# A decoder trunk on eight cores: the attention's first query tile in its second part, an earlier state load, and a background thread in single steps

## The chip, the cores and the metric

The kernel runs on the 8 cores of one Trainium2 chip. Each core takes one prompt of 2048 tokens and four sample sequences of 4 tokens (16 sample tokens), so the cores do the same work on different data and don't exchange anything. The metric is the device time of one launch, that of the slowest core, in microseconds; lower is better.

Engines: TensorE (PE) multiplies matrices and writes PSUM, which has 8 banks of 128 partitions x 512 fp32 numbers. ScalarE (ACT) and VectorE (DVE) read PSUM and SBUF. GpSimd (POOL) does small arithmetic here and issues DMAs that convert fp32 to bf16 or gather rows; SyncE (SP) only issues DMAs. Each engine works through its own instructions in order and waits on semaphores for the others.

## The reference, cut to what matters

Four layers follow each other: short gated convolution (A0), sparse attention (B), a gated recurrence (C), and a short convolution again (A1). Every layer is `x = LayerNorm(ALPHA * x + mixer(x))`.

```
# short conv: h, b, c, z = split(x @ w_in)
conv, new_buf = causal_dwconv(c_gate * h, buf, conv_w)   # buf: conv states
return (silu(z) * b_gate * conv) @ w_out, new_buf

# attention, per query block: three branches of keys
o_c = softmax(q k_c) v_c      # keys compressed by 32
o_s = softmax(q k_s) v_s      # the 16 blocks of 64 with the highest scores
o_w = softmax(q k_w) v_w      # the last 512 keys
y = ((g0*o_c + g1*o_s + g2*o_w) * silu(z)) @ w_out
```

For the sample tokens the compressed and selected keys come from a paged cache of 8192 rows per sequence. The results are the two outputs, the new key and value rows, and the new states.

## The kernel before, in words

**Order and dependencies.** The program is written out in order, and a small framework (`FW`) adds the waits. Every tile has one or more `Buf` records with its last writer and its readers; `FW.op` and `FW.dma` make the issuing engine wait for whatever an instruction reads or overwrites. A second DMA that writes under the same `Buf` therefore waits on its queue until the first has landed. Weights come through a ring of three tiles of 8 x 128 x 512 (`wtile`, `_issue_w`), loaded by POOL as soon as the tile that held the slot is used up.

**Layer A (`layer_A`).** For each of 8 column blocks c, and each of 4 token tiles of 512 and a small one of 16, TensorE computes four products (L560), each into a bank that `ps()` hands out in rotation: seven banks in A0, since bank 7 belongs to the page compression. ScalarE copies or activates two of them (L566, L567), VectorE does the convolution (L583 to L591). At the head of the layer `st_in`, the conv states (`sconv`, 32 KB), is loaded by SP, and ScalarE copies it into `exs` by eight instructions (L542), its first ones in the program. In A0 the generator `compress_pages` runs along: 32 pages of the sample cache are gathered by POOL into two buffers `PG` (L627), multiplied on VectorE with the weight table `WT` (L640) and summed on TensorE (L651, L653). Its setup code, which runs when the generator is made, puts four loads on the queues; that of `WT` (`s_cWT`) is held back on SP until the fourth tile of x (`xb[(0, 3)]`) has landed.

**Layer B, projections (`b_project`)** leave the queries in `G`, head pair c in `G[:, c, :]`: head c of group g=0 on partitions 0 to 63, of g=1 on 64 to 127.

**Layer B, attention (`b_attention`).** The work is a list of items. Part `ph` = 0 has query tiles QT = 0 and 1, part 1 has 2 and 3; in each part c runs over the 8 head pairs, and for each c the units (QT, g) run in the order (0,0) (0,1) (1,0) (1,1), or (2,0) (2,1) (3,0) (3,1). A unit's keys are cut into banks of 512 columns by `unit_banks`, and two banks are one item. The units have 3, 3, 7, 6 and 9, 8, 11, 10 items, so a c has 19 items in part 0 and 38 in part 1. For an item `scores` issues the products of keys and queries (L1251, L1244 for the compressed keys, L1255 for masks) into one of two PSUM pairs, and ScalarE takes the exponential of up to 1024 columns (L1260). Two items later `outputs` multiplies with the values (L1308) into the third or fourth pair, `psum2[2 + u % 2]` for the unit's number u. At a unit's end VectorE normalises from PSUM (L1331 to L1342). When g is 1, four transposes (L1346) into the same pair follow three items later, and VectorE copies them to `G` (L1348), over the queries that are used up. In part 0 an item "imp" is put in after the third item of (1,0) for each c (and one more at c = 6): scores of the compressed keys for 128 queries of tiles 2 and 3, and on VectorE the choice of the 16 best blocks (`importance`, L1272 to L1292). At c = 7 the item "nmt" transposes the eight results into masks, and four DMAs put them into the mask rows of the part-1 query tiles.

**Query tiles.** `QA[s_][g]`, with s_ = 2*ph + c%2, holds for one c the queries of a part (copied from `G` by SP), constants (`qc`, by POOL, converting) and the mask rows. `load_q` for the next c is emitted at the start of each c.

**Layer B, after the attention.** The z products: 8 blocks m x 5 token tiles (L933), Silu on ScalarE (L939), product into `G` on VectorE (L941). A second generator, `sample_bg`, does the sample tokens' attention in the background. `pump(k)` runs k of its steps, which issue their instructions at that place of the program. It has 181 steps: 20 to prepare (queries L1428 to L1435, compressed scores L1443 to L1462, block choice L1465 to L1479), then for 40 pieces in turn transposes (L1501, first half), scores of the piece before (L1520 to L1528) with an exponential (L1529), transposes (second half), values of the piece before (L1547, L1550). The two transposes of a piece share one bank, emptied by VectorE (L1503). The z stage runs two steps after each large tile, the output projection (`out_proj_ln`) five after each half of a row block.

**Output projection and LayerNorm (`out_proj_ln`).** For 17 row blocks i of 128 tokens: 16 matmuls in two halves h (L418), residual sum on VectorE (L428), square sum on ScalarE (L435), small operations on POOL, normalisation on ScalarE two blocks later (L448), scale and shift on VectorE (L453, L454), cast (L462), transposes on TensorE (L475) in two halves, which in layer B share one bank, and their copies to the next layer's input (L488 on ScalarE, L490 on VectorE).

The functions that the diff touches:

## Time and profile before

| | us |
|---|---|
| runs before (3) | 2170.76, 2172.91, 2248.44; median 2172.91 |
| profiled execution | 2175.07, span of its slowest core 2174.0 |
| spans of the 8 cores | 2142.8 to 2174.0, granted clock 0.886 to 0.901 |
| PE busy | 1699.6 (78%) |
| DVE busy | 1152.3 (53%) |
| ACT busy | 1100.9 (51%) |
| POOL busy | 356.0 (16%) |

The profile is that of core 2, the slowest. Stages in its time: A0 to about 411, projections of B to 540, attention to 1083 (part 0 to 766), z stage to 1216, output projection to 1446, then C and A1. "Granted clock" is the share of full speed that TensorE was given. Busy time of PE includes the drain of each matmul, so it is not work at the peak rate. An idle time in square brackets stands before the instruction, with what ended it.

In what follows part 1 is the code's `ph` = 0 and part 2 its `ph` = 1.

### The profile page before, as it was taken

To read this page: it belongs to the slowest core of one execution; us is meant where nothing else is said; L and a number is where in the kernel's file an instruction comes from. 1 tells how busy PE (TensorE), PEld (TensorE's weight loads), DVE (VectorE), ACT (ScalarE), POOL (GpSimd) and SP (SyncE) were. 2 spreads that over 40 slices of the span, in tenths; PEclk is the share of its full clock that TensorE was granted. 3 is DMA by queue.
4 is the path that set the end of the run, shared out by engine and by line. 5 is a ranking of instruction groups with operands and counts; after the bars stand their busy time and mean duration, and the time that the engine had idled before them with its cause. 6 is when DMAs were issued, how large, how long until landed. Compare 5 with 4: busy or idle time off the path is not lost.

```text
span 2174.0 us, 41364 instructions; the slowest of 8 cores (2142.8 to 2174.0 us)
## 1 busy us (share of the span) xinstructions
PE 1699.6 (78%) x13175; PEld 899.6 (41%) x13175; DVE 1152.3 (53%) x2070; ACT 1100.9 (51%) x1630; POOL 356.0 (16%) x660
## 2 busy tenths in 40 slices
PE   2799898788777688888848876669555368999996
PEld 1354454344545465555524433324221123444443
DVE  0687878630565632232224444431688888455568
ACT  0221117533666599999835423343888747211235
POOL 1011106410000000000011233220000046000026
PEclk8899999889898899999969987779877587789998
DMA  9367746564000000000074675133010144314226
GB/s 154 103 177 202 228 131 204 150 135 81 13 16 16 15 19 9 13 13 9 2 164 79 103 155 122 69 115 63 1 20 1 21 139 154 61 20 117 40 64 211
DMA packets 56118, 185.29 MB, mean 85 GB/s; under 512 B 10000, under 2 KB 19552, under 8 KB 47136
## 3 DMA queue, kind: packets, MB, share of 16 engines
q0 software_dynamic: 25024, 97.36, 22.7%
q1 hardware_dynamic: 30880, 85.28, 12.0%
q8 instruction: 109, 1.79, 0.3%
q14 instruction: 105, 0.86, 0.1%
HBM read 203.20 MB, written 40.83 MB: 112 GB/s over the span
## 4 chain that ended last, share of the span: by engine, by line
PE 56%; DVE 13%; ACT 12%; issue 9%; DMA 6%; POOL 3%; DVEq 1%; ACTq 0%; POOLq 0%; SPq 0%
PE pq L560 21%; PE pq L418 7%; PE pq L1251 7%; ACT s_bp_pt L1260 4%; PE pq L1308 4%; PE pq L718 3%; PE pq L1122 2%; PE pq L933 2%; DVE s_c_uc L788 2%; DMA s_XH<-xT 2%; DVE s_R L853 1%; PE pq L1255 1%; ACT s_bp_pc L1260 1%; ACT s_R L448 1%; PE pq L749 1%
## 5 line engine op out<-in xcount | busy, mean ns | idle before, releaser
L560 PE MATMUL pq<-s_XH,s_ring 128*128 128x512 bf16 (+1 forms) x2560 | 489.0, 350 | 62.6 <-ACT s_a_t L566 30.3
L1260 ACT ACTIVATE s_bp_pt<-pq 128x1024 bf16<-128x1024 f32 (+3 forms) x424 | 395.8, 973 | 58.5 <-PE pq L1308 46.9
L560 PEld LDWEIGHTS pq<-s_XH,s_ring 128*128 128x128 bf16 x2560 | 219.2, 100 | 321.0 <-issue 135.1
L418 PE MATMUL pq<-s_ring,s_G 128*128 128x512 bf16 (+1 forms) x1088 | 280.6, 418 | 23.8 <-DVE s_R L428 14.6
L1251 PE MATMUL pq<-s_bp_qa,s_bp_ks 128*128 128x512 bf16 (+3 forms) x640 | 201.7, 358 | 30.4 <-ACT s_bp_pt L1260 15.0
L418 PEld LDWEIGHTS pq<-s_ring,s_G 128*128 128x128 bf16 (+1 forms) x1088 | 111.4, 105 | 165.1 <-issue 80.0
L1331 DVE TENSOR_SCALAR s_bp_sm<-pq 128x12 f32<-128x12 f32 x64 | 10.8, 169 | 316.0 <-PE pq L1308 313.7
L567 ACT ACTIVATE s_a_t<-pq 128x512 f32<-128x512 f32 (+1 forms) x80 | 41.1, 514 | 269.0 <-PE pq L560 165.8
L1308 PE MATMUL pq<-s_bp_v,s_bp_pt 128*128 128x65 bf16 x3168 | 173.1, 198 | 0.7 <-ACT s_bp_pt L1260 0.7
L1308 PEld LDWEIGHTS pq<-s_bp_v,s_bp_pt 128*128 128x128 bf16 x3168 | 149.4, 100 | 41.3 <-issue 5.5
L1255 PE MATMUL pq<-s_bp_tri 128*128 128x128 bf16 x704 | 141.9, 226 | 0.0
L807 PE MATMUL pq<-s_c_ub,s_ring 128*128 128x512 bf16 (+1 forms) x160 | 55.5, 492 | 104.3 <-ACT s_c_aa L817 101.3
L1251 PE MATMUL pq<-s_bp_qa,s_bp_kw 128*128 128x512 bf16 x448 | 122.6, 314 | 17.8 <-ACT s_bp_pt L1260 16.8
L583 DVE TENSOR_TENSOR s_a_ext<-pq,s_a_t 128x512 f32<-128x512 f32 x64 | 44.1, 689 | 169.4 <-PE pq L560 113.3
L435 ACT ACTIVATE s_junk<-s_R 128x1024 bf16<-128x1024 f32 (+1 forms) x68 | 71.8, 1055 | 119.6 <-DVE s_R L428 119.4
L788 DVE SCALAR_TENSOR_TENSOR s_c_uc<-s_c_ext,s_vecs,s_c_uc 128x512 f32<-128x512 f32 x96 | 70.7, 750 | 89.6 <-ACT s_c_uc L779 82.8
L428 DVE SCALAR_TENSOR_TENSOR s_R<-s_R,pq 128x1024 f32<-128x1024 f32 (+1 forms) x68 | 82.5, 1214 | 56.0 <-PE pq L475 24.7
L475 PE MATMUL pq<-s_identb,s_xc 128*128 128x128 bf16 (+1 forms) x408 | 38.6, 240 | 91.0 <-ACT s_xc L462 56.6
L112 POOL DMA_DIRECT2D s_bp_qa<-qc x32 | 15.6, 491 | 481.7 <-PE pq L1308 471.5
L448 ACT ACTIVATE s_R<-s_R,s_st 128x1024 f32<-128x1024 f32 (+1 forms) x68 | 83.8, 1232 | 9.6 <-POOL s_st L441 8.8
L454 DVE TENSOR_TENSOR s_R<-s_R,s_btab 128x1024 f32<-128x1024 f32 (+1 forms) x68 | 83.6, 1229 | 7.3 <-DVE s_R L453 0.7
L453 DVE TENSOR_TENSOR s_R<-s_R,s_gtab 128x1024 f32<-128x1024 f32 (+1 forms) x68 | 82.9, 1219 | 8.3 <-ACT s_R L448 7.9
(279 smaller groups left out, 2820.3 us busy)
## 6 DMA issues: line engine op xcount, KB each, us to landing
s_ring<-wt POOLq DMA_DIRECT2D x35, 1024.0 KB, 10.3
xres<-s_R SPq DMA_DIRECT2D x48, 512.0 KB, 3.4
s_R<-xres SPq DMA_DIRECT2D x48, 512.0 KB, 5.9
s_R<-xt SPq DMA_DIRECT2D x16, 512.0 KB, 4.8
yt<-s_R SPq DMA_DIRECT2D x16, 512.0 KB, 3.5
s_XH<-xT POOLq DMA_DIRECT2D x4, 1024.0 KB, 23.7
s_bp_qa<-s_G SPq DMA_DIRECT2D x32, 128.0 KB, 2.2
rowsT<-s_bp_stg SPq DMA_DIRECT2D x12, 256.0 KB, 7.1
```

Of the source, the lines that this page charges most:

```text
L418: fw.op("pe", lambda e: e.matmul(self.psum2[pi][0:n, h * 512:h * 512 + 512], lhsT=self.G[:, k, t0:t0 + n], rhs=w[:, k, :], start=(k == 0), ...
L428: fw.op("dve", lambda e: e.scalar_tensor_tensor(out=R[0:n, :], in0=R[0:n, :], scalar=ALPHA, in1=self.psum2[pi][0:n, :], op0=ALU.mult, op1= ...
L435: fw.op("act", lambda e: e.activation(out=jk[0:n, :], in_=R[0:n, :], func=AF.Square, accum_out=st[0:n, 1:2]), reads=[Rb], writes=[jkb, sb_ ...
L448: fw.op("act", lambda e: e.activation(out=R[0:n, :], in_=R[0:n, :], func=AF.Identity, scale=st[0:n, 5:6], bias=st[0:n, 6:7]), reads=[Rb, s ...
L453: fw.op("dve", lambda e: e.tensor_tensor(out=R[0:n, :], in0=R[0:n, :], in1=gt[0:n, :], op=ALU.mult), reads=[Rb, gtb], writes=[Rb])
L454: fw.op("dve", lambda e: e.tensor_tensor(out=R[0:n, :], in0=R[0:n, :], in1=bt[0:n, :], op=ALU.add), reads=[Rb, btb], writes=[Rb])
L560: fw.op("pe", lambda e: e.matmul(p_[:, 0:n], lhsT=w[:, k, q * 128:(q + 1) * 128], rhs=self.XH[:, k, t0:t0 + n], start=(k == 0), stop=(k == ...
L788: fw.op("dve", lambda e: e.scalar_tensor_tensor(out=uc, in0=sh[r], scalar=self.vecs[:, cw + r * 8 + m:cw + r * 8 + m + 1], in1=uc, op0=ALU ...
L1251: fw.op("pe", lambda e: e.matmul(ps_[:, off:off + n * 128], lhsT=lhsT, rhs=rhs, start=(pi == 0), stop=(mask is None and pi == len(bank) - 1)),
L1255: fw.op("pe", lambda e: e.matmul(ps_[:, mo:mo + 128], lhsT=tri[:, mask * 128:mask * 128 + 128], rhs=identb, start=False, stop=(pi == len(b ...
L1260: fw.op("act", lambda e: e.activation(out=pt[:, 0:ncols], in_=ps_[:, 0:ncols], func=AF.Exp), reads=pbs[0:len(it["banks"])], writes=[ptb])
L1308: fw.op("pe", lambda e: e.matmul(ps_[:, col:col + 65], lhsT=lhsT, rhs=rhs, start=st, stop=(left[(u, qi // 2)] == 0)), reads=[lb, vb], writ ...
```

## The change

It does three things, and resizes what they need.

- `st_in` is made and loaded before the generator of the page compression, so that its DMA comes ahead of that generator's loads on the SP queue.
- The attention's units are put in another order: part 1 has (1,0) (1,1), part 2 has (2,0) (0,0) (3,0) (0,1) (2,1) (3,1). Query tiles of part 1 shrink to 512 columns, those of part 2 grow to 1536, and a part-2 load is two pieces. Four buffers instead of two hold the compressed scores' exponentials (`PC`) and the outputs (`OT`), by query tile.
- The sample thread is run in single steps between matmuls: in the z stage after the fourth and the eighth matmul of a large tile, from block m = 1 on, and in the output projection after every second matmul.

```diff
@@ out_proj_ln, yproj @@
                 for k in range(8):
                     fw.op("pe", ... matmul ...)
-                if bg and i < 16:
-                    bg[0](5)
+                    if bg and i < 16 and k % 2 == 1:
+                        bg[0](1)
@@ layer_A @@
+            st_in = self.sb("a_stin", [128, 8, 8], F32, es)
+            stib = Buf()
+            fw.dma("sp", st_in[:, :, :], self.d_sconv[j]..., writes=[stib])
             gen = self.compress_pages(es) if j == 0 else iter(())
             self.ps_rot = list(range(7)) if j == 0 else list(range(8))
-            st_in = self.sb("a_stin", [128, 8, 8], F32, es)
...
-            fw.dma("sp", st_in[:, :, :], self.d_sconv[j]..., writes=[stib])
@@ layer_B, z stage @@
                         for k in range(8):
                             fw.op("pe", ... matmul ...)
+                            if m >= 1 and tt < 4 and k % 4 == 3:
+                                pump(1)
...
-                        pump(2)
@@ b_alloc @@
-        P["QA"] = [[sb(f"qa{s_}{g}", [128, 1024], BF16) for g in range(2)] for s_ in range(4)]
+        P["QA"] = [[sb(f"qa{s_}{g}", [128, 512 if s_ < 2 else 1536], BF16) for g in range(2)] for s_ in range(4)]
-        P["PC"] = [... for i in range(2)]
+        P["PC"] = [... for i in range(4)]
-        P["OT"] = [... for i in range(2)]
+        P["OT"] = [... for i in range(4)]
@@ b_consts @@
-        for s_ in range(2):
+        for s_ in range(4):
             for g in range(2):
-                fw.op("dve", ... memset(P["QA"][s_][g][self.ER[g], :], 0.0) ...)
+                fw.op("dve", ... memset(P["QA"][s_][g][self.ER[g], 0:512], 0.0) ...)
@@ load_q @@
+        parts = [(0, 512, 512)] if ph == 0 else [(0, 0, 512), (512, 1024, 1024)]
         for g in range(2):
             kr = self.KR[g]
             qb = P["qb"][s_][g]
-            fw.dma("pool", P["QA"][s_][g][self.CR[g], :], self.d_qc[..., ph * 1024:ph * 1024 + 1024], writes=[qb[1]])
-            fw.dma("sp", P["QA"][s_][g][kr, :], self.G[kr, c, ph * 1024:ph * 1024 + 1024], ..., writes=[qb[0]])
+            for o, t0, n in parts:
+                fw.dma("pool", P["QA"][s_][g][self.CR[g], o:o + n], self.d_qc[g * 8 + c, :, t0:t0 + n], writes=[qb[1]])
+                fw.dma("sp", P["QA"][s_][g][kr, o:o + n], self.G[kr, c, t0:t0 + n], ..., writes=[qb[0]])
@@ b_attention @@
+        order = [[(1, 0), (1, 1)], [(2, 0), (0, 0), (3, 0), (0, 1), (2, 1), (3, 1)]]
...
-                for QT in (2 * ph, 2 * ph + 1):
-                    for g in range(2):
+                for QT, g in order[ph]:
+                    if True:
...
-                                it["cmp"] = P["PC"][(u // 2) % 2]
+                                it["cmp"] = P["PC"][QT]
...
-            qo = (QT % 2) * 512
+            qo = (0, 0, 512, 1024)[QT]
...
-            ot, otb = P["OT"][(u // 2) % 2]
+            ot, otb = P["OT"][QT]
```

The mask copies at "nmt" go to columns 512 to 1535 of the part-2 tiles. Everything else is unchanged.

## Rows read from the trace of the kernel before

**Rows 1.** Timeline of the start: start us, us, engine line op; idle before, releaser.
```profile
20.24 14.33 PE L560 MATMUL pq<-s_XH,s_ring 128*128 128x512 bf16 x56 [20.24 <-DMA s_ring<-wt]
...
40.69 0.33 SPq L112 DMA_DIRECT2D s_cWT<-twt  x1
41.06 0.94 SPq L112 DMA_DIRECT2D s_a_stin<-sconv  x1
62.06 1.28 ACT L542 ACT_TABLE_LOAD   x1 [62.06 <-DMA s_a_stin<-sconv]
...
85.36 15.01 PE L560 MATMUL pq<-s_XH,s_ring 128*128 128x512 bf16 x61 [1.82 <-DVE s_a_t L590]
```
**Rows 2.** Busy time by stage: window, us, busy us of engines, PEclk, DMA share, GB/s.
```profile
540.00:766.00 226.00, 165.83 (x1975) 116.01 (x1976) 128.76 (x371) 143.09 (x156) 7.80 (x16) 0.86 0.08 15
766.00:1079.00 313.00, 274.56 (x3655) 185.33 (x3652) 89.73 (x214) 292.37 (x313) 5.87 (x12) 1.00 0.06 11
```
**Rows 3.** Timeline of part 1, first matmuls of (0,0), (1,0), next (0,0).
```profile
625.54 0.60 PE L1244 MATMUL pq<-s_bp_qa,s_bp_kca 128*128 128x512 bf16 x2
635.08 0.67 PE L1244 MATMUL pq<-s_bp_qa,s_bp_kca 128*128 128x512 bf16 x2
...
655.42 0.85 PE L1244 MATMUL pq<-s_bp_qa,s_bp_kca 128*128 128x512 bf16 x2
```
**Rows 4.** Waits of part 1 (us, times, longest); timeline and group of VectorE there.
```profile
PE pq L1308 <- DVE s_G L1348: 21.8, 7, 3.2
PE pq L1308 <- DVE s_bp_sm L1331: 20.8, 7, 3.2
...
671.69 0.69 DVE L1272 TENSOR_TENSOR s_bp_stg<-s_bp_e 128x512 f32<-128x512 f32 x1 [1.07 <-ACT s_bp_e L1218]
...
679.45 0.69 DVE L1348 CAST s_G<-pq 128x512 bf16<-128x512 f32 x1
...
L1337 DVE TENSOR_TENSOR s_bp_stg<-pq,s_bp_sm 128x768 f32<-128x768 f32 x63 | 60.3, 958 | 7.3 <-DVE s_bp_sm L1335 1.3
```
**Rows 5.** After the attention: timeline of TensorE, busy time, and waits of 1112 to 1216.
```profile
1111.96 0.26 PE L1445 MATMUL pq<-s_sg_sb,s_sg_sa 32*128 32x128 bf16 x1 [17.93 <-DMA s_sg_sb<-tsb]
...
1162.06 1.90 PE L933 MATMUL pq<-s_XH,s_ring 128*128 128x512 bf16 x8
...
1112.00:1216.00 104.00, 89.65 (x678) 45.54 (x679) 40.98 (x96) 63.15 (x85) 9.03 (x10) 0.94 0.51 92
...
PE pq L1501 <- DVE s_sg_kt L1503: 6.4, 8, 2.0
```
**Rows 6.** Output projection of B: busy time, waits from 1256 us, timeline of VectorE.
```profile
1257.00:1386.00 129.00, 91.45 (x755) 49.75 (x755) 57.21 (x87) 41.35 (x62) 38.10 (x60) 0.79 0.53 123
...
PE pq L475 <- ACT s_xc L462: 17.6, 8, 3.1
...
1404.40 1.22 DVE L428 SCALAR_TENSOR_TENSOR s_R<-s_R,pq 128x1024 f32<-128x1024 f32 x1 [4.52 <-PE pq L475]
...
1412.90 1.22 DVE L428 SCALAR_TENSOR_TENSOR s_R<-s_R,pq 128x1024 f32<-128x1024 f32 x1 [3.96 <-PE pq L475]
```
**Rows 7.** DMAs of the start: page table (last: us to landing); two weight loads.
```profile
s_cpti<-ptabr SPq DMA_DIRECT2D x1, 16.0 KB, 3.2
...
L112 POOL DMA_DIRECT2D s_ring<-wt x2: 536/538/541, 7.3 to 7.8; - x2
...
DMA to landing us min/median/max: 45.8/45.8/45.8
```
**Rows 8.** Page compression: VectorE's product (ns; first, last start), its waits 85 to 320.
```profile
L640 DVE TENSOR_TENSOR s_cPRD<-s_cPG,s_cWT x32: 2283/2291/2293, 87.5 to 304.9; 128x2048 bf16<-128x2048 f32 x32
...
DVE s_cPRD L640 <- DMA s_cPG<-kvpool,s_cidx: 22.5, 9, 6.4
```
**Rows 9.** Timeline of part 2: POOL's last q load, first matmuls of a unit after.
```profile
1002.50 0.49 POOL L112 DMA_DIRECT2D s_bp_qa<-qc  x1 [9.62 <-PE pq L1308]
...
1040.53 0.61 PE L1244 MATMUL pq<-s_bp_qa,s_bp_kca 128*128 128x512 bf16 x2 [0.22 <-ACT s_bp_pt L1260]
```

More of the change, by code:

```diff
@@ L532, in T_ @@
                 return r
+            st_in = self.sb("a_stin", [128, 8, 8], F32, es)
+            stib = Buf()
+            fw.dma("sp", st_in[:, :, :], self.d_sconv[j].rearrange("p (c q) -> p c q", c=8), writes=[stib])
             gen = self.compress_pages(es) if j == 0 else iter(())
             self.ps_rot = list(range(7)) if j == 0 else list(range(8))
-            st_in = self.sb("a_stin", [128, 8, 8], F32, es)
             st_out = self.sb("a_stout", [128, 8, 8], F32, es)
             cap_t = self.sb("a_cap", [128, 8, 2], F32, es)
-            stib, stob = Buf(), [Buf() for _ in range(8)]
+            stob = [Buf() for _ in range(8)]
             capb = [Buf() for _ in range(8)]
-            fw.dma("sp", st_in[:, :, :], self.d_sconv[j].rearrange("p (c q) -> p c q", c=8), writes=[stib])
             for c in range(8):
@@ L978, in b_alloc @@
         P["kcbdb"] = Buf()
-        P["QA"] = [[sb(f"qa{s_}{g}", [128, 1024], BF16) for g in range(2)] for s_ in range(4)]
+        P["QA"] = [[sb(f"qa{s_}{g}", [128, 512 if s_ < 2 else 1536], BF16) for g in range(2)] for s_ in range(4)]
         P["qb"] = [[[Buf() for _ in range(3)] for g in range(2)] for s_ in range(4)]
         P["PT"] = [(sb(f"pt{i}", [128, 1024], BF16), Buf()) for i in range(4)]
-        P["PC"] = [(sb(f"pc{i}", [128, 1024], BF16), Buf()) for i in range(2)]
+        P["PC"] = [(sb(f"pc{i}", [128, 1024], BF16), Buf()) for i in range(4)]
         P["STG"] = [(sb(f"stg{i}", [128, 768]), Buf()) for i in range(5)]
         P["stgi"] = 0
-        P["OT"] = [(sb(f"ot{i}", [128, 4, 128], BF16), Buf()) for i in range(2)]
+        P["OT"] = [(sb(f"ot{i}", [128, 4, 128], BF16), Buf()) for i in range(4)]
         P["SM"] = [(sb(f"sm{i}", [128, 16]), Buf()) for i in range(2)]
@@ L1013, in b_consts @@
             fw.dma("pool", P["KCA"][g][ar, :, :], self.d_kcaug[g].rearrange("p (q n) -> p q n", q=4), writes=[P["kcab"][g]])
-        for s_ in range(2):
+        for s_ in range(4):
             for g in range(2):
-                fw.op("dve", lambda e: e.memset(P["QA"][s_][g][self.ER[g], :], 0.0), writes=[P["qb"][s_][g][2]])
+                fw.op("dve", lambda e: e.memset(P["QA"][s_][g][self.ER[g], 0:512], 0.0), writes=[P["qb"][s_][g][2]])
         fw.dma("pool", P["KB4"][0][:], self.d_kb4.rearrange("p (v n) -> p v n", v=2), writes=[P["KB4"][1]])
@@ L1135, in load_q @@
             qb = P["qb"][s_][g]
-            fw.dma("pool", P["QA"][s_][g][self.CR[g], :], self.d_qc[g * 8 + c, :, ph * 1024:ph * 1024 + 1024], writes=[qb[1]])
-            fw.dma("sp", P["QA"][s_][g][kr, :], self.G[kr, c, ph * 1024:ph * 1024 + 1024],
-                   reads=[self.gb[(c, 2 * ph)], self.gb[(c, 2 * ph + 1)]], writes=[qb[0]])
+            for o, t0, n in parts:
+                fw.dma("pool", P["QA"][s_][g][self.CR[g], o:o + n], self.d_qc[g * 8 + c, :, t0:t0 + n], writes=[qb[1]])
+                fw.dma("sp", P["QA"][s_][g][kr, o:o + n], self.G[kr, c, t0:t0 + n],
+                       reads=[self.gb[(c, tt)] for tt in range(t0 // 512, (t0 + n) // 512)], writes=[qb[0]])
     @staticmethod
@@ L1183, in b_attention @@
                             if gi == 0:
-                                it["pt"] = P["PC"][(u // 2) % 2] if g == 0 else None
-                                it["cmp"] = P["PC"][(u // 2) % 2]
+                                it["pt"] = P["PC"][QT] if g == 0 else None
+                                it["cmp"] = P["PC"][QT]
                             items.append(it)
@@ L1227, in scores @@
                     for g in range(2):
-                        fw.dma("sp", P["QA"][s_][g][self.ER[g], :], nm[self.ER[g], :], reads=[nmb], writes=[P["qb"][s_][g][2]])
+                        fw.dma("sp", P["QA"][s_][g][self.ER[g], 512:1536], nm[self.ER[g], :], reads=[nmb], writes=[P["qb"][s_][g][2]])
                 return
```

## The prediction

> **What bounds the kernel now.** I read the page first: TensorE is busy 78% of the span, VectorE and ScalarE about half, so no engine fills it and the answer is in the stages. Then I read a timeline or a table of busy time at each of the three places that the diff touches.
>
> *The first 85 us.* [rows 1] is the timeline of the start. TensorE runs 56 matmuls from 20.24 us, which fills the seven PSUM banks it may use, and then waits for ScalarE, which has done nothing yet: its first instruction waits until 62.06 us for the small table of conv states. The reason stands on the SP queue: the table is issued at 41.06 us, right behind the weight table of the page compression (40.69), whose issue waits for the fourth tile of x. The second column block starts at 85.36 us.
>
> *The attention.* [rows 2] shows two regimes. In part 2 (766 to 1079 us) ScalarE is busy 292.37 of 313 us at a granted clock of 1.00, so the exponentials bound it: 304 items in 313 us, 1.03 each. In part 1 it is busy 143.09 of 226, at a clock of 0.86. The first matmuls of the units there [rows 3] give the period of a head pair c: 29.88 us (625.54 to 655.42), of which the two units of query tile 0 take 9.54. The stalls are in [rows 4]: twice per c TensorE waits about 3 us for a PSUM pair, once behind the two short units (21.8 us in 7 waits), once in tile 1 (20.8 in 7), where the copy that frees the pair, L1348, is queued on VectorE behind the importance scores.
>
> *After the attention.* [rows 5]: one z tile has run when the sample thread's matmul waits until 1111.96 us for its constants. From 1112 to 1216 us TensorE is busy 89.65 of 104. In the output projection [rows 6] the eight row blocks between 1257 and 1386 us take 16.1 us each at a clock of 0.79; the last ones, with the thread used up, 8.50 (1404.40 to 1412.90).
>
> **The early states.** The change puts the state load on the SP queue right behind the two loads of the setup. It costs one issue (0.94 us at most) ahead of the page table, which moves the first gather by that much; nobody waits for it. A 16 KB load issued there lands in 3.2 us [rows 7], so ScalarE is ready before the first bank is full. TensorE then runs through the first column block: 128 matmuls, 56 in 14.33 us and 72 more at 15.01/61, the pace of the second block [rows 1]: 20.24 + 14.33 + 17.7 = 52.3, and a small tile. The fourth x tile is there at 40.69. The next block needs its weights: issued at 7.3 us with 45.8 to landing [rows 7], 53.1. So it starts 85.36 - 53.1 = 32.3 us earlier. Less 2: VectorE's product for the first gathered page stands at the head of that block, can hardly start before the page lands (the transfers of the start run to 62 us), takes 2.28 us [rows 8], and frees the ninth tile's bank that much later. Bounds: 25 if the whole layer hangs on the chain of gathers (87.5 to 62), 34 if tiles and weights are each a little faster. VectorE waited only 22.5 us for gathers in the layer [rows 8], so I take **30**.
>
> **The first query tile among long units.** Removed from part 1: six items per c, 8 x 9.54 = 76 us, with one of the two stalls in them. The clock of 0.86 says that part 1 spends 28% of its time at the lower of the two levels (1.2 GHz), and in the timeline that is the 4 us behind each stall; half of that goes too, where TensorE then bounds the items, some 0.6 us each: 5 more. The other stall stays: now the copy for (1,1) is queued behind the importance scores of the next c, with the same seven items before the pair is used again. Added to part 2: per c 11 banks, 5.5 full exponentials, 5.7 us at 1.03; with more masks per bank I take 6.2, so 50 us. VectorE is busy 89.73 of 313 there, so the extra normalisations lie beside it. At the transition the last importance scores are 6 items ahead of the transposes that need them, and were 12: 7.8 us of scores (671.69 to 679.45 [rows 4]) and a queued normalisation against 6.3, 3 us once. Net 76 + 5 - 50 - 3 = **28** (bounds: 18 without the clock and at 7 us per c, 38 if the second stall goes too).
>
> The q loads: part 1 issues 32 as before, of half the size, part 2 64 in place of 32, on both queues. The second piece waits on its queue for the first to land, since both write under one name. Nothing else is queued there in the attention but the four mask copies. A load is issued when TensorE has left the slot, a whole c ahead: POOL issues at 1002.50 for units that start at 1040.53 [rows 9]. Two landings of some 3 us, like the small one of [rows 7], cost nothing in 38. Memsets (8 of half the size for 4) and buffers: nothing.
>
> **The spaced sample steps.** The thread has 181 steps. Before, 64 went into the z stage and the rest in fives after each half row block. Now it is 56 (none in the first z block) and 128.
> - z stage: four z tiles and a small one, not one, run before the wait that ends at 1111.96; the wait itself stays, the constants' DMA is where it was. 4 x 1.75 (a tile of 8 is listed with 1.90, its end overlapping [rows 5]) + 0.4 = 7.5 us. Eight steps leave for later: 89.65 less 31 tiles of 1.75 over 62 steps is 0.57 each, 4.6. Of the 14.35 us idle after 1112 the transposes' waits for the copy go (6.4 in 8), since four matmuls lie between two steps, and perhaps 1 of the rest. Sum 19: it ends at about 1197.
> - output projection: the thread has period four (transposes, values, transposes, scores) and eight steps per block keep its phase. Step 57 is a transpose step, so every half block ends on *scores*. Behind them ScalarE, in order, has an exponential, the normalisation and the cast before TensorE may transpose. That is the longest of the waits on L462, 3.1 us; their mean was 17.6/8 = 2.2 [rows 6]. Per block: 16.1 - 1.1 for two steps fewer - 1.3 for waits inside a group of five + 0.9 = 14.6 for 13 of them and 8.5 for the first three: 215 against 205 (1216 to 1421). The four blocks that ran at 8.5 carry pages too. So 10 lost.
>
> Net **9**; bounds -20 (every block at 17) and +30 (the spacing keeps the clock up and the exponential runs under the transposes).
>
> **Sum.** 30 + 28 + 9 = 67 off the profiled execution's 2175.07 (span 2174.0): 2108. The median shown, 2172.91, is 2 below; I say **2106**. A measurement of this kernel tells 2% from no change, 43.5 us: faster means under 2129.4.
>
> **Rivals.**
> - *Spacing pays in full (0.17).* For: the waits inside a group are latencies that two matmuls cover in part, and the clock of 0.79 comes with stalls. Against: the ScalarE chain at the block's end. 30 in place of 9: 2085.
> - *The row blocks stall (0.16).* Blocks at 17 us (-20), 20 for the attention, 28 at the start: gain 28, about 2145. For: the steps' phase above.
> - *Slower than before (0.04).* In part 2 the short units sit between long ones that share a PSUM pair: (2,0) and (3,0) with only the three items of (0,0) between, likewise (3,0) and (2,1). If VectorE frees the pair late, TensorE stalls there as in part 1, 3 us and 1.5 at the lower clock, 16 times: 72 us. Then 28 becomes -44, and with stalling blocks too the sum is 30 - 44 - 20: 2207. It decides at a delay of 1.2 us: three items take 3.1, the normalisation until its last read of PSUM the 0.96 of L1337 [rows 4] and three small operations, 1.9. Against: VectorE has no long queue in part 2.
> - *The states don't come early (0.04).* If the load's packets waited behind x until 40.7 us, 7 of the 30 go: 2113.
> - *A lower clock (0.03).* Denser matmuls on eight cores could lower it. TensorE needs 274.56/304 = 0.90 us per item in part 2 at 1.00; at the 0.79 of [rows 6] it would need 1.14 and bound it: 350 x 0.11 = 38 us, 2144. Against: the densest long stretch of before is the one at 1.00. The Trainium skill ("TensorE: Matmul & The Clock Gate", in "Seeing it yourself") states that dense matmuls on three cores of a die bring the die to 13/16 of the clock; by that an item would need 1.11 and the sum would be 2134. The row of 1.00 does not agree.
>
> The forecast itself has 0.56, with 2085 to 2129 as its own range.
>
> **Numbers.** Faster: 0.56 + 0.17 + 0.04 = 0.77. Within 2%: 0.16 + 0.03 and half of the slower rival, 0.21. Slower by over 2%: the other half, 0.02. The range runs from 2076, 9 below the first rival, to 2144.
>
> **What would show it.** ScalarE's first state copy before 10 us and the second column block at 53 (50 to 60). Part 1 at 145 to 155 us with one 3 us wait per c; part 2 at 355 to 365 with ScalarE over 90% busy and no wait of TensorE over 1 us. After it the same wait for the constants, no wait for L1503, and in the output projection some 3 us on L462 in every block. I am wrong if the second column block hangs on gathers, if part 2 shows waits on L1308, or if the blocks take 12 us or 17.

## The result, and the profile after

| | us |
|---|---|
| runs before beside them (4) | 2170.76, 2172.91, 2174.39, 2248.44 |
| runs after (4) | 2094.84, 2100.99, 2107.79, 2116.99; median 2104.39 |
| ratio to before | 0.967, 95% interval 0.962 to 0.972: faster |
| predicted | 2106 (2076 to 2144) |
| profiled execution | 2094.84, span of its slowest core 2093.1, clock 0.899 to 0.918 |

The ratios here and below are formed from undisturbed runs (here without 2248.44 and 2116.99), so the one of an experiment is not always the quotient of two medians.

The first markers of each stage (medians over the 8 cores, from the timelines) give the place of the change. The attention is cut at its mask item, which has three items of c = 7 ahead of it and ten behind it in part 1.

| stage | before | after | difference |
|---|---|---|---|
| start to the projections of B | 411.1 | 379.2 | -31.9 |
| projections of B | 120.6 | 122.2 | +1.6 |
| attention to the mask item | 222.3 | 135.1 | -87.2 |
| mask item to the attention's end | 320.9 | 376.7 | +55.8 |
| z stage to the constants' landing | 27.5 | 28.7 | +1.2 |
| rest of the z stage | 104.9 | 91.6 | -13.3 |
| output projection of B | 233.1 | 235.5 | +2.4 |
| C and A1 | 712.6 | 708.2 | -4.4 |

C and A1 are the same code in all kernels here and measured 708.2 to 713.3 in them, so the last line is no effect of the change. Nor is the +1.2 ahead of the constants' landing: it comes from subtracting medians. The cores fall into two groups there, and taken within each core the stretch is 23.6 to 29.3 us before and 22.8 to 30.1 after, median 27.2 and 26.4. Within each core the output projection goes from 232.6 to 235.3.

The start, timeline of core 2 (start us, us, engine line op; idle before, releaser), against [rows 1]:

```profile
1.97 0.43 SPq L112 DMA_DIRECT2D s_a_stin<-sconv  x1
...
5.05 1.28 ACT L543 ACT_TABLE_LOAD   x1 [5.05 <-DMA s_a_stin<-sconv]
...
21.69 30.06 PE L561 MATMUL pq<-s_XH,s_ring 128*128 128x512 bf16 x158 [21.69 <-DMA s_ring<-wt]
...
53.80 8.36 PE L561 MATMUL pq<-s_XH,s_ring 128*128 128x512 bf16 x38 [2.05 <-DVE s_a_t L591]
```

ScalarE starts at 5 us, TensorE runs through the first column block, and the second starts at 53.8, as forecast; the wait there ends with VectorE's convolution and not with its weights.

Busy time of core 2 by stage (window, us, busy us of engines, clock granted to TensorE, DMA share, GB/s), against [rows 2, 5, 6]: parts 1 and 2, the z stage after its wait, the output projection:

```profile
500.00:650.00 150.00, 111.58 (x1345) 79.66 (x1368) 88.46 (x273) 104.45 (x113) 9.76 (x20) 0.89 0.10 19
650.00:1012.00 362.00, 307.83 (x4193) 217.43 (x4274) 132.94 (x318) 330.26 (x354) 11.75 (x24) 1.00 0.06 12
1042.00:1134.00 92.00, 76.33 (x596) 39.14 (x607) 36.34 (x85) 53.90 (x74) 8.12 (x9) 0.96 0.52 96
...
1134.00:1369.00 235.00, 157.65 (x1271) 86.57 (x1294) 112.48 (x165) 83.08 (x122) 63.35 (x125) 0.82 0.50 111
```

Part 1 takes 150 us and part 2 362, ScalarE busy 91% of it. [rows 2] cut the attention of before at 766 us, which is some 8 us too early: the first scores of part 2 stand at 773.74 there and at 651.37 now (core 2).

```profile
773.74 0.71 PE L1244 MATMUL pq<-s_bp_qa,s_bp_kca 128*128 128x512 bf16 x2
...
651.37 0.38 PE L1249 MATMUL pq<-s_bp_qa,s_bp_kca 128*128 128x512 bf16 x1 [0.35 <-issue]
```

From first scores to first scores, part 1 fell from 233.5 us (540.25 to 773.74) to 151.3 (500.08 to 651.37), which is 82, and part 2, up to the first z product, grew from 309.6 to 360.3, which is 51. The table's cut at the mask item gives 87 and 56 for the same change. TensorE's waits in four stretches (us in total, times, longest), against [rows 4 to 6]: 500 to 640, 640 to 1013, 1042 to 1134, 1134 to 1369 us.

```profile
PE pq L1313 <- DVE s_bp_sm L1336: 17.8, 6, 3.1
...
PE pq L1351 <- DVE s_bp_ot L1347: 6.1, 5, 3.2
...
PE pq L1506 <- DVE s_sg_kt L1508: 10.8, 8, 1.5
...
PE pq L475 <- ACT s_xc L462: 37.7, 13, 3.1
PE pq L475 <- ACT s_XH L488: 19.7, 16, 3.0
```

Of part 1's two stalls per c one is left, as forecast (L1313, 3 us). The timeline of core 2 shows its cause at c = 6, the copy that stands behind the last operation of the importance on VectorE:

```profile
624.60 0.18 DVE L1297 TENSOR_SCALAR s_bp_nq<-s_bp_wk 128x32 f32<-128x32 f32 x1
...
624.84 0.69 DVE L1353 CAST s_G<-pq 128x512 bf16<-128x512 f32 x1
...
625.68 0.37 PE L1313 MATMUL pq<-s_bp_vc,s_bp_pc 64*128 64x65 bf16 x4 [2.89 <-DVE s_bp_sm L1336]
```

In part 2 TensorE waits at most 0.4 us for VectorE to free a PSUM pair; its one wait over 1 us behind the transition, 3.2 us on L1351, is for the very last transposes of the attention. In the z stage the waits for the copy of the sample's transposes, which I had written off, have grown from 6.4 us to 10.8. In the output projection each of 13 blocks waits 2.9 us on average on L462, as forecast, and then about 1 us on L488.

### The profile page after: what moved, and what is told of

Its sections match the earlier page's. It is cut to its first block, busy times and chain, and to the rows that moved or that the text cites. A ratio compares the mean times of both kernels' runs of the same rounds, so it can differ in the third digit from the quotient of the medians.

```text
span 2093.1 us, 40663 instructions; the slowest of 8 cores (2065.4 to 2093.1 us)
## 1 busy us (share of the span) xinstructions
PE 1690.5 (81%) x13175; PEld 895.8 (43%) x13175; DVE 1152.3 (55%) x2074; ACT 1093.4 (52%) x1626; POOL 349.5 (17%) x676
## 4 chain that ended last, share of the span: by engine, by line
PE 58%; ACT 13%; DVE 12%; issue 9%; POOL 3%; DMA 3%; DVEq 0%; ACTq 0%; SPq 0%; POOLq 0%
PE pq L561 20%; PE pq L1256 7%; PE pq L418 7%; PE pq L1313 4%; ACT s_bp_pt L1265 4%; PE pq L1124 3%; PE pq L719 3%; DVE s_c_uc L789 2%; PE pq L934 2%; PE pq L1045 1%; DVE s_R L854 1%; ACT s_bp_pc L1265 1%; ACT s_xc L462 1%; PE pq L1552 1%; PE pq L1260 1%
## 5 line engine op out<-in xcount | busy, mean ns | idle before, releaser
L561 PE MATMUL pq<-s_XH,s_ring 128*128 128x512 bf16 (+1 forms) x2560 | 469.5, 341 | 33.4 <-DMA s_ring<-wt 21.4
L561 PEld LDWEIGHTS pq<-s_XH,s_ring 128*128 128x128 bf16 x2560 | 214.7, 98 | 276.8 <-issue 46.6
L418 PE MATMUL pq<-s_ring,s_G 128*128 128x512 bf16 (+1 forms) x1088 | 296.6, 418 | 23.8 <-DVE s_R L428 14.5
L1313 PE MATMUL pq<-s_bp_v,s_bp_pt 128*128 128x65 bf16 x3168 | 170.3, 196 | 0.7 <-ACT s_bp_pt L1265 0.7
L418 PEld LDWEIGHTS pq<-s_ring,s_G 128*128 128x128 bf16 (+1 forms) x1088 | 104.2, 104 | 140.8 <-issue 69.6
L1313 PEld LDWEIGHTS pq<-s_bp_v,s_bp_pt 128*128 128x128 bf16 x3168 | 146.6, 99 | 40.1 <-issue 3.0
L808 PE MATMUL pq<-s_c_ub,s_ring 128*128 128x512 bf16 (+1 forms) x160 | 55.1, 490 | 103.0 <-ACT s_c_aa L818 99.9
L1256 PE MATMUL pq<-s_bp_qa,s_bp_kw 128*128 128x512 bf16 (+1 forms) x448 | 118.7, 305 | 18.7 <-ACT s_bp_pt L1265 18.4
L1336 DVE TENSOR_SCALAR s_bp_sm<-pq 128x12 f32<-128x12 f32 x64 | 10.8, 169 | 209.5 <-PE pq L1313 205.2
L112 POOL DMA_DIRECT2D s_bp_qa<-qc x48 | 23.5, 490 | 427.3 <-PE pq L1313 384.7
L1508 DVE CAST s_sg_kt<-pq 128x512 bf16<-128x512 f32 x68 | 46.9, 689 | 81.2 <-PE pq L1506 78.8
```

The lines of the kernel that those rows point to most:

```text
L418: fw.op("pe", lambda e: e.matmul(self.psum2[pi][0:n, h * 512:h * 512 + 512], lhsT=self.G[:, k, t0:t0 + n], rhs=w[:, k, :], start=(k == 0), ...
L561: fw.op("pe", lambda e: e.matmul(p_[:, 0:n], lhsT=w[:, k, q * 128:(q + 1) * 128], rhs=self.XH[:, k, t0:t0 + n], start=(k == 0), stop=(k == ...
L1256: fw.op("pe", lambda e: e.matmul(ps_[:, off:off + n * 128], lhsT=lhsT, rhs=rhs, start=(pi == 0), stop=(mask is None and pi == len(bank) - 1)),
L1313: fw.op("pe", lambda e: e.matmul(ps_[:, col:col + 65], lhsT=lhsT, rhs=rhs, start=st, stop=(left[(u, qi // 2)] == 0)), reads=[lb, vb], writ ...
```

## Experiments: the change in its parts

The texts written before these runs count their times from 2172.9 us. The kernel before, run beside the experiments, took 2158 to 2163, so the absolute times come out lower than expected, and only ratios and stages are compared.

**The states alone.** In the kernel before, the load of `st_in` is placed ahead of `compress_pages`; nothing else.

> The kernel before with the early load of the conv states alone. My theory: everything between the first column block and the projections of B moves 32 us earlier, and the rest of the program is unchanged, so the time is 2172.9 - 31 = 2142 (2136 to 2148), ratio 0.986. Rival: the layer was also held up by the gathers and the shift is partly given back in B and C, because weights and residuals come later than they are wanted; then the time is 2150 or more.

Measured: 2129.95 against 2157.96 for the kernel before beside it, ratio 0.986 (0.983 to 0.988): 31 us (here and below, what the ratio leaves off 2158). The projections of B start at 379.7, the value of the full change, and all later stages keep their lengths (attention 542.3, before 543.2). My theory holds; nothing is given back.

**The attention alone.** The new order, `QA`, `PC`, `OT`, memsets and loads, without the other two parts.

> The kernel before with the attention's new order and its buffers alone. My theory: part 1 loses 87 us and part 2 gains 56, as the markers of the full change show, so the attention is 31 us shorter and the time 2142 (2134 to 2150). Rival: the 87 us of part 1 were partly a gift of the earlier start or of another clock; then part 1 alone loses the 81 that I had summed up or less, and the time is 2150 or more.

Measured: 2123.35, ratio 0.984 (0.982 to 0.987): 34 us. Stages 134.2 and 376.0, so -88.1 and +55.1: the gain is the order's own and owes nothing to the earlier start.

**The spaced steps alone.** `pump(1)` after every fourth matmul of a large z tile from m = 1 and `bg[0](1)` after every second of the projection, in the kernel before.

> The kernel before with the spaced sample steps alone, in the z stage and in the output projection. My theory: z stage 12 to 14 us shorter from its start to its end, output projection 2 to 4 us longer, together 9 to 11 off: 2163 (2156 to 2170), ratio 0.995. Rival: the output projection before was longer only because of its fives, and single steps alone pay 30 in full: 2143.

Measured: 2147.35, ratio 0.996 (0.994 to 0.999): 8 us. The rest of the z stage is 91.6 (104.9 before), the output projection 234.2 (233.1). The product of the three ratios is 0.967, that of the full change: within the intervals the three parts are independent, 31, 34 and 8 us.

## Experiments: what still stalls

From here on every kernel is the changed one with one edit, and its stages are compared with the column "after". The ratios are still those to the kernel before, where the changed kernel has 0.967.

**The steps one slot later.**

```diff
-                            if m >= 1 and tt < 4 and k % 4 == 3:
+                            if m >= 1 and tt < 4 and k % 4 == 3 and 2 * ((m - 1) * 4 + tt) + k // 4 >= 1:
```

> The changed kernel with the first z step of the sample thread left out, so that every later step comes one slot later: each half row block now ends on the first transposes of a piece in place of its scores (55 + 128 slots still hold all 181 steps). My theory: a block is 14.1 us because the exponential, the normalisation and the cast stand one behind the other on ScalarE before TensorE may transpose (3.1 us on L462 in each of 13 blocks). With the last scores two matmuls earlier, or four with the fourth step between, the exponential is done before the normalisation is due: the wait falls to 1 to 2 us, the output projection from 235 to 210 to 225 us, the time by 10 to 25 us. Rival: what closes the block is the chain of sums, square and copies whatever the step, and the wait stays at 3 us: no change within 5 us.

Measured: ratio 0.961 (0.960 to 0.963). The output projection falls by 3.4 us only, to 232.1. Its waits, 1119 to 1351 us of core 2:

```profile
PE pq L475 <- ACT s_XH L488: 36.7, 15, 3.3
PE pq L475 <- DVE s_XH L490: 12.7, 8, 2.3
PE pq L475 <- ACT s_xc L462: 7.1, 6, 2.7
```

The wait on L462 went, as my theory had it (37.7 to 7.1), and came back as one on L488 (19.7 to 36.7) and on L490: the rival is right. A seam of that kernel shows what closes a block, whatever the step:

```profile
1245.36 1.22 DVE L428 SCALAR_TENSOR_TENSOR s_R<-s_R,pq 128x1024 f32<-128x1024 f32 x1 [2.27 <-PE pq L418]
...
1245.96 0.38 PE L475 MATMUL pq<-s_identb,s_xc 128*128 128x128 bf16 x4 [0.78 <-ACT s_xc L462]
...
1247.02 1.06 ACT L435 ACTIVATE s_junk<-s_R 128x1024 bf16<-128x1024 f32 x1 [1.31 <-DVE s_R L428]
...
1248.07 0.58 ACT L488 ACTIVATE s_XH<-pq 128x512 bf16<-128x512 f32 x1
...
1248.80 0.38 PE L475 MATMUL pq<-s_identb,s_xc 128*128 128x128 bf16 x4 [2.45 <-ACT s_XH L488]
```

The block's last matmul releases the residual sum (1.22), that the square sum (1.06), behind which on ScalarE stands the copy (0.58) that frees the one bank for the second half's transposes. TensorE waits through it: 0.78 + 2.45 here, 3.08 + 0.84 at a seam of the changed kernel.

By its stages the kernel is 16 us faster than the changed one, 13 by the ratios, within the 10 to 25 that I had said, but for another reason: the rest of the z stage falls from 91.6 to 79.1, with no wait on L1506 left. That was not expected.

**The z product behind the copy.**

```diff
+                            if k == 3 and held:
+                                product()
...
-                        fw.op("dve", ... tensor_tensor(out=gsl, in0=gsl, in1=sz[:, 0:n], op=ALU.mult) ...)
+                        held.append((m, tt, sz, szb))
```

> The changed kernel with VectorE's product of a z tile issued only after the fourth matmul of the next tile, so behind the copy of the sample's transposes and not ahead of it. My theory: the waits for that copy that stayed in the z stage (10.8 us in 8 on L1506) come from VectorE's order: the product waits for the Silu, the Silu for the exponential and two table loads of 1.28 us, and the copy is queued behind it. They go, and the z stage is 8 to 11 us shorter. Rival: the copy itself is late behind the transposes, or TensorE then waits for a free bank in place of it: 3 us or less.

Measured: ratio 0.963 (0.961 to 0.964), rest of the z stage 83.5: 8.1 us. The waits on L1506's counterpart halve (5.6 in 4). The chain in the changed kernel, timeline of core 2:

```profile
1083.75 1.28 ACT L1534 ACT_TABLE_LOAD   x1 [3.07 <-PE pq L1533]
...
1085.05 0.60 ACT L1534 ACTIVATE s_sg_pt<-pq 128x512 bf16<-128x512 f32 x1
1085.66 1.28 ACT L942 ACT_TABLE_LOAD   x1
...
1086.95 1.08 ACT L942 ACTIVATE s_b_z<-pq 128x512 f32<-128x512 f32 x2
...
1087.65 0.69 DVE L944 TENSOR_TENSOR s_G<-s_G,s_b_z 128x512 bf16<-128x512 bf16 x1 [4.74 <-ACT s_b_z L942]
1088.26 0.68 DVE L1508 CAST s_sg_kt<-pq 128x512 bf16<-128x512 f32 x1
...
1089.10 0.38 PE L1506 MATMUL pq<-s_identb,s_sg_kv 128*128 128x128 bf16 x4 [1.50 <-DVE s_sg_kt L1508]
```

Exponential, table load, Silu, product, copy: the copy has its input early (the transposes before it end at 1084.87) and is queued behind a product that waits 4.74 us. In either edit this copy goes ahead of the product. In the kernel with the steps one slot later:

```profile
1085.17 0.69 DVE L1508 CAST s_sg_kt<-pq 128x512 bf16<-128x512 f32 x1 [1.26 <-PE pq L1506]
...
1087.79 0.69 DVE L944 TENSOR_TENSOR s_G<-s_G,s_b_z 128x512 bf16<-128x512 bf16 x1 [1.93 <-ACT s_b_z L942]
```

That two different edits which change this order take the wait away, one wholly and one by half, confirms the order on VectorE as the cause. Of a table switch the row shows 1.29 us from load to activation (1085.66 to 1086.95). The Trainium skill ("ScalarE: Activation LUTs", "What ACT_TABLE_LOAD costs") gives 1283 ns for the load and about 1380 ns of drain with it, 2.66 us in all; the load agrees with the row, a drain does not show in it.

**Importance two items later.**

```diff
-                            if QT == 1 and gi == 2:
+                            if QT == 1 and gi == 4:
```

> The changed kernel with the importance item (and the mask item) two items later, after the fifth item of unit (1,0) and not after the third. My theory: the wait left in part 1 (17.8 us in 6 on L1313 for the PSUM pair) comes from VectorE's queue: the copy of (1,1) stands behind 7 us of importance. With the item two later the copy goes first; what stands behind the importance then is the normalisation of (1,0), whose pair is not used again for six items. The wait goes: 3 us for each of six c and some 1 at the lower clock, 15 to 30 us off. Rival: the importance delays another hand-over of a pair by the same amount, and the wait only changes its place: within 6 us. At the transition the mask item comes later by the same two items, so nothing is lost there by either.

Measured: ratio 0.964 (0.962 to 0.965). To the mask item 130.4 us (-4.7, with two items more in it), from there 371.5 (-5.2, with two fewer): 10 together. The wait on L1313 is gone, and one on the normalised outputs is there, 500 to 632 us of core 2:

```profile
PE pq L1351 <- DVE s_bp_ot L1347: 18.0, 7, 8.0
```

Neither theory had it right: the wait moved, and yet 10 us went (8 by the ratios), where I had said 15 at least and the rival 6 at most. The 8.0 is the second importance at c = 6, now just ahead of a unit's end.

**Importance at unit (1,1).**

```diff
-                                if g == 0 and c < 7:
+                                if g == 1 and c < 7:
                                     items.append(dict(kind="imp", i=c))
-                                if g == 1 and c == 6:
+                                if g == 0 and c == 6:
```

> The changed kernel with the importance item moved by seven items, to the third item of unit (1,1), where VectorE has just been given the normalisation of (1,0) and is next wanted for that of (1,1), 5 items later. My theory: part 1 is bound by when VectorE hands over, and the place counts: two items later moved the wait (18.0 us in 7 on L1351 for the normalised outputs in place of 17.8 in 6 on L1313) and gained 5 us in part 1; here the 7 us of importance fit between the two normalisations but for about 1.5 us, and part 1 falls from 135 to 118 to 127 us. Rival: VectorE's work per c, 13 of 16.9 us, is close enough to a bound that any place makes somebody wait 2 to 3 us: part 1 at 130 or more.

Measured: ratio 0.971 (0.969 to 0.973); to the mask item 141.7 us, 6.6 more than after. The rival holds. The timeline of VectorE (core 2) tells why my "7 us" was too small: 

```profile
569.47 0.69 DVE L1277 TENSOR_TENSOR s_bp_stg<-s_bp_e 128x512 f32<-128x512 f32 x1 [1.00 <-ACT s_bp_e L1223]
...
577.53 0.17 DVE L1336 TENSOR_SCALAR s_bp_sm<-pq 128x12 f32<-128x12 f32 x1
...
580.58 0.58 PE L1351 MATMUL pq<-s_bp_tri,s_bp_ot 128*128 128x128 bf16 x4 [3.98 <-DVE s_bp_ot L1347]
```

The importance holds VectorE for 8.1 us, and the transposes wait 3.98 for the normalisation behind it.

**The constants ahead of the gathers.**

```diff
-        gather(0)
-        gather(1)
         SA, SAb = ld("sa", ...)
...
+        gather(0)
+        gather(1)
         gather(2)
```

> The changed kernel with the three loads of the sample thread's constants issued by POOL ahead of the first two gathers. My theory: the 17.2 us for which TensorE waits on L1450 come from POOL's order, for the first gather waits 8 us for its index, and from the 3.5 MB of residual rows that SP issues meanwhile; issued at 1013 the constants land in 3 to 5 us, before the first step that needs them, and the z stage is 14 to 18 us shorter. Rival: the loads still share the DMA engines with the residual rows and the gathers and land some 20 us after their issue, or the first page is then what is late: 6 us or less.

Measured: ratio 0.961 (0.959 to 0.963). From the z stage's start to the matmul that needs the constants 13.4 us in place of 28.7 by the medians, or of 26.4 within each core: 13 to 15 us off, the ratios say 13, and no wait for a DMA in it. Of SP's residual rows 3.5 MB are issued from 1018 to 1026 us in the changed kernel, and POOL's first gather only at 1020.82 with the constants behind it; queue order cost what the forecast had left alone. The edit puts the constants ahead of the gathers and of the residual rows at once (they are issued before 1028.3 us, the rows from 1028.62), so which of the two had held them is not shown.

**The transposes in the middle and at the end of a block.**

```diff
+            late = bg and 4 <= i < NT + 4
+            def mid():
+                turn(i - 4, 0)
+                evac(i - 4, 0)
...
+            if late:
+                turn(i - 4, 1)
```

`yproj` calls `mid` between its two halves. The old calls `turn(i - 3, 0)`, `evac(i - 3, 0)` and the early `turn(i - 4, 1)` stay for layers without a thread.

> The changed kernel with the transposes of layer B's output projection moved: both halves of a row block go through their one bank one after the other across a seam of blocks, of which the second waits for the first's copy (L488), that for the square sum (L435) and that for the residual sum behind the block's last matmul (L428). Here the first half is transposed and copied in the middle of the block after next, the second half at its end. My theory: this chain, 2.5 to 3 us at every seam, is what sets the block's time, and the sample step only chooses which of its members is met; so 13 to 16 waits of 3 us on L488 and most of those on L462 go, the output projection falls from 235 to 185 to 205 us and the time by 30 to 50 us. Rival: the sample's exponentials and copies then stand in the same way on ScalarE and VectorE in the middle of the block, and half of it or more comes back as waits on L488 and L490 there: 15 us or less.

Measured: 2061.23, ratio 0.955 (0.953 to 0.958). The output projection takes 206.7 us, 28.8 less (209.4 and 26 less within each core; it varies from 204.9 to 215.6 over the cores). Its waits, 1128 to 1336 us of core 2:

```profile
PE pq L1518 <- DVE s_sg_kt L1520: 25.4, 10, 2.9
...
PE pq L477 <- ACT s_xc L464: 4.6, 2, 2.8
```

The waits on L462 and L488 (here L464, L490) fall from 57 us to under 10: the seam was the bound. Part comes back in the middle of the blocks, as the rival had it, but as 25.4 us of waits for the sample's copy on VectorE and not on L488 and L490, so the gain ends just under my 30 to 50.

## Experiments: the edits together

**Four edits** (one slot later, constants, importance two items later, transposes moved).

> The changed kernel with four edits together: the sample's steps one slot later, its constants loaded ahead of the gathers, the importance two items later, and the transposes of layer B's output projection in the middle and at the end of a block. Theory: they lie in different stages (10 in the attention, 27 in the z stage, 3 and 30 to 50 in the output projection) and add up: 65 to 85 us under the changed kernel, a ratio of 0.93 to 0.94 to the kernel before. Rival: the z stage's two gains overlap, or the clock falls with the denser work, and half of it is left: 0.945 or more.

Measured: 2005.47, ratio 0.928 (0.926 to 0.931) to the kernel before, 0.960 times that of the changed one. Attention 9.9 us less than after, z stage 27.6, output projection 44.2 (191.3): 82. The first two are the sums of the single edits (10; 12.5 + 15.3). The third is 12 more than 3.4 + 28.8. The waits for the sample's copy are off its list, and 23.0 us in 14 for the sample's exponential, none over 1.9, stand there: moved transposes and the later slot help each other. Part 2 and output projection of core 2:

```profile
653.00:1014.00 361.00, 317.75 (x4262) 216.06 (x4259) 132.84 (x318) 329.42 (x354) 11.74 (x24) 1.00 0.06 12
...
1104.00:1294.00 190.00, 141.24 (x1308) 77.60 (x1307) 111.34 (x166) 81.70 (x120) 79.09 (x126) 0.90 0.61 138
```

The clock in the output projection is 0.90 where it was 0.82. Opening the seam alone had not done that: with only the transposes moved it is 0.82 to 0.86, by core, and with only the later slot 0.80 to 0.82. So part of the 12 us may be clock; no run separates it from the order of the work.

**Two more edits in part 1.** In the four-edit kernel the eighth importance item goes to the very start, and in part 1:

```diff
-                post.append((step + 3, transposes))
+                post.append((step + (5 if it["ph"] == 0 else 3), transposes))
```

> The kernel with the four edits, and in part 1 of the attention two more: the eighth importance item stands at the very start (after the first item of c = 0) in place of just before the end of a unit, and the transposes of part 1 come five items after the normalisation is issued in place of three. My theory: the waits left in part 1 (18.8 us in 11 on the normalised outputs, one of 7.9) are VectorE's lateness and nothing else, and both edits give it slack: part 1 falls from 130 to 113 to 122 us. Rival: VectorE's own work, 76 of 130 us, and the exponentials, 96 of 130, alternate badly, and the time lost comes back as waits for a PSUM pair: part 1 stays at 126 or more.

Measured: runs of 2022.33, 2026.71, 2063.49 and 2078.23, for which no ratio is given; even the fastest is 17 us above the four-edit kernel. The stage speaks clearly: 150.4 us to the mask item against 130.1. TensorE's wait at one c:

```profile
600.55 0.69 DVE L1365 CAST s_G<-pq 128x512 bf16<-128x512 f32 x1
...
601.15 0.16 DVE L1348 TENSOR_SCALAR s_bp_sm<-pq 128x12 f32<-128x12 f32 x1
...
601.38 0.38 PE L1325 MATMUL pq<-s_bp_vc,s_bp_pc 64*128 64x65 bf16 x4 [4.96 <-DVE s_bp_sm L1348]
```

My theory fell. The rival has the right wait, 29.6 us in 6 for a PSUM pair, but not its cause or size: the transposes two items later put their copy (L1365) behind the importance again. What counts here is not slack but on which side of the importance the copy stands in VectorE's queue. The other edit, the eighth importance at the start, was not run by itself.

**Steps three slots later**, the four-edit kernel with 3 in place of 1.

> The kernel with the four edits, but the sample's steps three slots later than in the changed kernel and not one (53 + 128 slots for the 181 steps). Each half row block then has values, transposes, scores, transposes, and the values wait for an exponential across a seam of two halves. My theory: the 23.3 us in 15 waits for the sample's exponential in the output projection are a matter of distance, two steps as before but with four more transposes between: they fall to 12 or less and the output projection from 191 to 180 to 188 us. Rival: ScalarE works off the copy, the normalisation, the cast and the square first at each seam, so the exponential is done no earlier and the values wait as long or longer: 191 or more.

Measured: 2011.43, ratio 0.932 (0.929 to 0.935); output projection 195.4 us. The waits for the exponential leave the list of the longest, and others take their place, 1090 to 1290 us of core 2:

```profile
PE pq L1516 <- DMA s_sg_kv<-kvpool,s_sg_idx: 12.0, 5, 4.3
PE pq L1585 <- DVE s_sg_kt L1518: 8.7, 3, 3.9
```

The gathered pages come late (each gather is issued when the values of its buffer are done) and VectorE's copy with them. The rival's number holds, by a mechanism that it did not name. The rest of the z stage is 4 us shorter than in the four-edit kernel (74.7 against 78.8) and the output projection 4 longer. The four-edit kernel stays the fastest by its median, but the two intervals overlap.

## Why the prediction was right

The sum was 67 off 2175.07, hence 2108, and 2106 for the median; measured 2104.39. The hit is closer than its terms: the ratio says 71 us, the stages 73 (32 + 31 + 10), and the median of four runs holds one of 2116.99. By its steps:

- **Start, 30: 32 measured, alone 31.** ScalarE before 10 us, TensorE through the first block, second block at 53.8 with 53 forecast. What ends the wait there is VectorE and not, as in the working, the weights; when these landed no row shows.
- **Attention, 28: 31 measured, alone 34.** Part 1 150 us (145 to 155 said), part 2 362 (355 to 365 said), ScalarE 91% busy. One 3 us wait per c is left, and it is VectorE's queue: its place in the list alone moves it (three kernels). Of the transition's 3 us the two waits of 1.8 and 1.6 us are there. The 3 us that were off lie in part 1: 81 less the transition's 3 was said and 82 measured from first scores to first scores on core 2, while part 2 has 51 for 50. The forecast had read part 2 as 313 us for 304 items, cut too early; it is 309.6, 1.02 each, which changes the 50 by less than 1. "No wait of TensorE over 1 us" holds but for the 3.2 us at the attention's end.
- **Z stage, 19: 12 measured, the term that failed.** The tiles and steps moved out of it came as said: TensorE's busy time after the constants fell from 89.65 to 76.33 us, 13.3 for the 12.1 of the working. The idle time did not: 14.35 before, 15.67 after, where 7 were to go. "The transposes' waits for the copy go (6.4 in 8), since four matmuls lie between two steps": they grew to 10.8. I had counted TensorE's distance and not asked what the copy stands behind on VectorE. One slot later, or the product behind the copy, gives 8 to 12 us back.
- **Output projection, 10 lost: 2 lost by the medians, 5 on core 2, on which it was worked out.** I had 14.6 us for each of 13 blocks; on core 2 the residual sums of [rows 6]'s kind go from 1160.29 to 1345.20, 14.2 each. The 3.1 us wait on L462 came as forecast. Its reading as the thing that sets the block was wrong: taken away, another link of the same chain held TensorE, and moving the transposes gave 26 to 29 us.
- These two errors, 7 too much and 5 to 8 too little, cancel: 9 said for both, 10 by the stages, 8 alone. That the sum of the two came out is luck; the start and the attention are not.

**Rivals.** "Spacing pays in full" wanted 30 us and "row blocks stall" 20 lost; the spacing alone gave 8, and the blocks take 14.2 us and not 17. The slower one needed a late hand-over in part 2; no wait on L1313 of 1 us is there. The states did come early, with ScalarE's first instruction at 5.05 us. The lower clock did not come: in part 2 all eight cores show a granted clock of 0.99 or 1.00, the upper level of 2.4 GHz, with TensorE busy 85% of it on core 2. The 13/16 that the Trainium skill ("TensorE: Matmul & The Clock Gate", "Seeing it yourself") gives for a die with three cores on dense matmuls is not in these rows of part 2.

Left open: why the four-edit kernel's attention still takes 502 us where its items, at 1.03 us each, would take about 480. By core 2's timeline all of it lies in part 1: 141 us for 113 items, against 361 for the 352 of part 2. The largest part that the trace names there is 17.2 us in 7 waits of TensorE for the normalised outputs.

## What to carry to other kernels

When a wait is to be hidden by distance on one engine, read the other engine's queue first: a copy that is ready still stands behind whatever waits ahead of it, and an edit that only changes that order (one slot, two items) was worth 8 to 13 us here, as much as all of the spaced steps. A listed wait is the last link of its chain; before pricing its removal, ask which link TensorE would meet next, and break the chain at the resource it shares, here the one bank emptied across a block's seam.

## What the runs showed of the hardware

- A small load can be late behind what was issued ahead of it: 72 KB of constants, issued at 1025.59 us behind 3.5 MB of residual rows and two gathers, released TensorE 16 us later on core 2 and 11 us later on core 0 (1020.19 to 1030.90); issued ahead of both, it held nobody.
- A switch of ScalarE's table cost 1.29 us here, from its load's start to the next activation; with Silu and exponential alternating, 25 loads of 1.28 us, 32 us, lie in the 92 us after the constants.
- The granted clock of a stage moves with small edits, and not with its length alone: in the output projection 0.81 to 0.83 over the cores of the changed kernel, 0.82 to 0.86 with the transposes moved (26 us shorter), 0.89 to 0.91 with the four edits (44 us shorter).
